# Decoder layer on one core: the G pair of the z blocks moves into the half-product stage, and the convolution of branch C starts there

## What is computed

```python
h = rmsnorm(x, lp['norm_mix'])
z = h @ lp['w_in']
qa, ka, va, qb, fb, ib, gb, xc, gc, xd, gl = jnp.split(z, split_at, axis=-1)
o_a = stick_breaking(qa, k_all, v_all, pos0, lp['sb_bias'])
o_b, S_new = hgrn2(qb, fb, ib, gb, S0, lp)     # o * silu(gb)
o_c, h_new, conv_c_new = rg_lru(xc, gc, conv_c_hist, h0, lp)   # conv, gates, scan, * gelu(gc)
o_d, pool_new = pool_mixer(xd, pool_hist, pos0, lp)
gates = jax.nn.sigmoid(gl.reshape(B, L, N_BRANCH, D_MODEL))
x = x + jnp.sum(gates * proj, axis=2) @ lp['w_out']
```

## Time and profile before

| | |
|---|---|
| median of 3 runs | 1770.21 us (1769.98 to 1774.1) |
| the profiled execution | 1776.43 us |
| its span | 1774.6 us |
| PE busy | 1738.9 us (98%) |
| DVE, ACT, POOL busy | 63%, 41%, 44% |
| granted clock of TensorE, mean | 0.992 of full speed |

### The profile page before, as it was taken

The page is one execution under the profiler, slowest core; times in us unless marked ns, Lnnn a source line. Parts: engine busy times, 40 slices in busy tenths (PEclk is TensorE's granted clock), DMA queues, the critical chain, the costliest instruction groups (busy, mean ns, idle before and its releaser), DMA issues.

```text
span 1774.6 us, 30899 instructions
## 1 busy us (share of the span) xinstructions
PE 1738.9 (98%) x12865; PEld 1686.9 (95%) x12865; DVE 1112.9 (63%) x1255; ACT 730.9 (41%) x1034; POOL 777.4 (44%) x531
## 2 busy tenths in 40 slices
PE   8999999979999999999999999999999999999998
PEld 8999999978999978799999999999999999999998
DVE  6931111836857066657843976888888887775744
ACT  6423332354422266532334654444444443334521
POOL 1656674312222211112133287766777736668021
PEclk9999999989999999999999999999999999999999
DMA  6523326122222532447443222232322285334032
GB/s 226 75 94 111 120 77 215 49 80 66 69 79 80 172 109 93 139 148 260 168 148 111 107 97 98 97 110 103 119 100 97 98 300 184 136 116 146 25 123 97
DMA packets 84655, 214.80 MB, mean 121 GB/s; under 512 B 14851, under 2 KB 31779, under 8 KB 83363
## 3 DMA queue, kind: packets, MB, share of 16 engines
q1 hardware_dynamic: 73570, 189.48, 31.0%
q0 software_dynamic: 4032, 14.68, 2.7%
q10 hardware_dynamic: 6912, 8.65, 1.4%
HBM read 149.48 MB, written 63.40 MB: 120 GB/s over the span
## 4 chain that ended last, share of the span: by engine, by line
PE 90%; DVE 3%; ACT 3%; POOL 2%; DMA 1%; issue 1%; SPq 0%; ACTq 0%; POOLq 0%; DVEq 0%
PE ps L1632 24%; PE ps L1082 20%; PE ps L1069 11%; PE ps L1212 10%; PE ps L1680 10%; PE ps L1664 3%; PE ps L1300 2%; PE ps L1167 1%; PE ps L1385 1%; PE ps L1056 1%; PE ps L1109 1%; DMA masks<-in_wb 1%; PE ps L1549 1%; PE ps L1419 1%; PE ps L1406 1%
## 5 line engine op out<-in xcount | busy, mean ns | idle before, releaser
L3311 POOL TENSOR_TENSOR Wl<-BIG,Wh 128x512 fp32r<-128x512 f32 x110 | 142.9, 1309 | 117.9 <-ACT Wh L2182 117.9
L3166 POOL CAST Uh<-BIG 128x1024 fp32r<-128x1024 f32 x27 | 36.0, 1335 | 310.8 <-PE ps L1069 201.8
L2536 DVE TENSOR_TENSOR BIG<-BIG,ps 128x528 f32<-128x528 f32 x45 | 31.7, 704 | 159.5 <-PE ps L1212 159.5
L2960 DVE SCALAR_TENSOR_TENSOR ps<-BIG,fpar,ps 128x1023 f32<-128x1023 f32 x84 | 107.9, 1285 | 36.0 <-ACT ps L2273 35.1
L1069 PE MATMUL ps<-Hh,Uh 128*128 128x352 f32 x384 | 128.3, 334 | 0.8 <-ACT BIG L1923 0.8
L1069 PE MATMUL ps<-Hh,Ul 128*128 128x352 f32 x384 | 123.6, 322 | 0.0
L1069 PE MATMUL ps<-Hl,Uh 128*128 128x352 f32 x384 | 123.3, 321 | 0.0
L3263 POOL TENSOR_TENSOR Ul<-BIG,Uh 128x1024 fp32r<-128x1024 f32 x15 | 36.1, 2412 | 164.7 <-ACT Uh L2142 164.7
L1632 PE MATMUL ps<-Hl,Wh 128*128 128x264 f32 x528 | 107.1, 284 | 0.0
L1082 PE MATMUL ps<-Hh,Uh 128*128 128x352 f32 x432 | 96.7, 333 | 9.0 <-ACT BIG L1799 6.3
L2949 DVE TENSOR_TENSOR BIG<-BIG,ps 128x528 f32<-128x528 f32 x110 | 77.3, 703 | 42.8 <-PE ps L1632 36.9
(11 more groups left out here) (465 smaller groups left out, 5575.9 us busy)
## 6 DMA issues: line engine op xcount, KB each, us to landing
BIG<-in_wu SPq DMA_DIRECT2D x44, 512.0 KB, 4.6
hidden<-BIG SPq DMA_DIRECT2D x22, 528.0 KB, 2.7
late_gates<-BIG SPq DMA_DIRECT2D x18, 528.0 KB, 3.0
BIG<-sums SPq DMA_DIRECT2D x12, 792.0 KB, 4.8
BIG<-in_wgl SPq DMA_DIRECT2D x9, 1024.0 KB, 5.9
BIG<-in_wd SPq DMA_DIRECT2D x6, 1536.0 KB, 9.6
H<-late_gates SPq DMA_DIRECT2D x17, 528.0 KB, 3.7
gates<-BIG ACTq DMA_DIRECT2D x48, 176.0 KB, 2.1
```

The lines of the kernel that those rows point to most:

```text
L2960: link(v.scalar_tensor_tensor(y[:, back:SEQ], x[:, 0:SEQ - back], w, y[:, back:SEQ], ALU.mult, ALU.add), v.scalar_tensor_tensor(ys[:, :, b ...
L3311: nc.gpsimd.tensor_tensor(Wl[:, b], src, Wh[:, b].bitcast(F32), ALU.subtract).then_inc(S("w_lo"), 1)
```

## The change

- Blocks `GB0` and `GB1` are no longer made by `block_z`. Their weights are the second of now ten pairs (`Z_PAIR = 1`), without the sigmoid; they are stored in `late_gates` and loaded back into `Z` at the stage's end.
- The rows of XC come back into the place of GC (`conv_rows`) and not into that of FB. They are loaded after product T3 of the last pair, and DVE convolves the first row before it adds product T1 of that pair.
- The small tables (histories, `wpool`) lie in `FO` and are loaded while the stage begins. The rows of GC come back after both convolutions.
- ACT's `root(0)` and `gelu(0)` stand ahead of its copies of FB, and `turned_v(0)` ahead of `decay(1)`.
- POOL makes the split of `IB1` ahead of the first pair's seven low parts, not behind three of them.
- Behind the changed places `before()` and `VA0, VA1` keep their order on ACT: `before()` first.

```diff
-ZB = 14
+ZB = 12
+Z_PAIR = 1
-PAIRS = (4 * LATE - COVER) // 2
+PAIRS = (4 * LATE - COVER) // 2 + 1
-         "C10", "C11", "GB0", "GB1", "VA0", "VA1")
+         "C10", "C11", "VA0", "VA1")
...
             def pair_weights(c, sem):
+                if c == Z_PAIR:
+                    src = a["wz"][18:20]
...
+            for i in range(2):
+                sp.dma_start(phist[:, i], a["phist"][i]).then_inc(S("cd_in"), 16)
+            sp.dma_start(chist, a["chist"]).then_inc(S("cd_in"), 16)
+            sp.dma_start(ch0, a["ch0"]).then_inc(S("cd_in"), 16)
+            sp.dma_start(wpool, a["wpool"]).then_inc(S("cd_in"), 16)
...
             sp.wait_ge(*upto("gp_done", made(PAIRS - 1, T3)))
-            rows_back(1, Z[:, XD:XD + 2, :])
-            sp.wait_ge(*upto("gc_kept0", 32))
-            sp.wait_ge(*upto("gc_kept1", 32))
-            rows_back(2, Z[:, GC:GC + 2, :])
+            rows_back(0, conv_rows, on("gw_first"))
+            rows_back(1, Z[:, XD:XD + 2, :], on("gw_in1"))
+            sp.wait_ge(*upto("gp_done", 7 * PAIRS))
...
+            rows_back(3, turn, S("cd_in"))
...
+            sp.dma_start(Z[:, GB:GB + 2, :], late_gates[2 * Z_PAIR:2 * Z_PAIR + 2].rearrange("i p t -> p i t"))\
+                .then_inc(S("cd_in"), 16)
+            sp.dma_start(wrg, a["wrg"]).then_inc(S("cd_in"), 16)
             gate_out(PAIRS - 1, 0)
...
             gate_out(PAIRS - 1, 1)
...
+            sp.wait_ge(S("cd_ready"), 2)
+            rows_back(2, Z[:, GC:GC + 2, :], on("gw_in0"))
...
-            block_z("GB0", (0, lambda: turned_v(0, turn[:, 0], (2,))))
+            block_z("VA0", (0, lambda: turned_v(0, turn[:, 0], (2,))))
             turned_v(1, turn[:, 1], range(2))
-            block_z("GB1", (0, lambda: turned_v(1, turn[:, 1], (2,))))
-            block_z("VA0")
-            block_z("VA1")
+            block_z("VA1", (0, lambda: turned_v(1, turn[:, 1], (2,))))
...
             rates(0)
             decay(0)
+            root(0)
+            gelu(0)
             for i in range(2):
-                act.wait_ge(S("cd_ready"), i + 1)
                 z_out(f"FB{i}", FB[:, i])
...
-            root(0)
-            gelu(0)
             rates(1)
-            decay(1)
             act.wait_ge(S("pool_read"), 2)
             turned_v(0)
+            decay(1)
             root(1)
             gelu(1)
-            z_out("GB0", Z[:, GB, :])
             turned_v(1)
-            z_out("GB1", Z[:, GB + 1, :])
...
+            for c in range(PAIRS):
+                for part in (T2, T3, T1, T4, B22):
+                    if c == PAIRS - 1 and part == T1:
+                        dve.wait_ge(S("cd_in"), 80)
+                        dve.wait_ge(*upto("gw_first", 32))
+                        convolved(0)
+                    gate_sum(c, part)
+            convolved(1)
...
             split(4)
-            for part in LOWS[:3]:
-                gate_low(0, part)
             split(5)
-            for part in LOWS[3:]:
+            for part in LOWS:
                 gate_low(0, part)
```

More of the change, by code:

```diff
@@ L67 @@
 KA = XD
[L68 removed]
+Z_COLS = (1792, 2304, 2048, 1280, 768, 1024, 512, 256, 0, 1536)
 BRANCH_AT = (QA, GB, GC, XD)
@@ L239 @@
 USERS = ("XC0", "XC1", "XD0", "XD1", "GC0", "GC1", "IB0", "IB1", "QB0", "QB1", "C00", "C01", "FB0", "FB1", "D0", "D1",
-         "C10", "C11", "GB0", "GB1", "VA0", "VA1")
-RING = ("XD0", "XD1", "GC0", "GC1", "IB0", "IB1", "QB0", "QB1", "FB0", "FB1", "GB0", "GB1", "VA0", "VA1")
+         "C10", "C11", "VA0", "VA1")
+RING = ("XD0", "XD1", "GC0", "GC1", "IB0", "IB1", "QB0", "QB1", "FB0", "FB1", "VA0", "VA1")
 FRONT = RING.index("IB1") + 1
@@ L394, in program @@
         wrg = r.take(2, 2, P)
-        phist = r.take(2, DB, HIST)
         assert r.at <= R0 + RING_AT - 4 * T
@@ L701, in keep_rows, with rows_back @@
                 outs += 16
-            def rows_back(n, rows):
-                sp.dma_start(rows, early_rows[n].rearrange("i p t -> p i t")).then_inc(S("cd_in"), 16)
+            def rows_back(n, rows, signal):
+                sp.dma_start(rows, early_rows[n].rearrange("i p t -> p i t")).then_inc(signal, 16)
             keep_rows(0, XC)
@@ L743, in _ @@
             sp.wait_ge(*upto("gp_done", made(PAIRS - 1, T3)))
-            rows_back(1, Z[:, XD:XD + 2, :])
-            sp.wait_ge(*upto("gc_kept0", 32))
-            sp.wait_ge(*upto("gc_kept1", 32))
-            rows_back(2, Z[:, GC:GC + 2, :])
-            gate_out(PAIRS - 1, 0)
[L749 to L754, removed]
+            rows_back(0, conv_rows, on("gw_first"))
+            rows_back(1, Z[:, XD:XD + 2, :], on("gw_in1"))
+            sp.wait_ge(*upto("gp_done", 7 * PAIRS))
+            for i in range(2):
+                sp.wait_ge(*upto(f"gc_kept{i}", 32))
+            rows_back(3, turn, S("cd_in"))
+            for half in range(2):
+                sp.wait_ge(*upto(f"g_stored{half}", 16 * (Z_PAIR + 1)))
+            sp.dma_start(Z[:, GB:GB + 2, :], late_gates[2 * Z_PAIR:2 * Z_PAIR + 2].rearrange("i p t -> p i t"))\
+                .then_inc(S("cd_in"), 16)
+            sp.dma_start(wrg, a["wrg"]).then_inc(S("cd_in"), 16)
+            gate_out(PAIRS - 1, 0)
             gate_out(PAIRS - 1, 1)
[L756 to L759, removed]
+            sp.wait_ge(S("cd_ready"), 2)
+            rows_back(2, Z[:, GC:GC + 2, :], on("gw_in0"))
             z_wait("D0")
@@ L814, in gate_in @@
                 i, u = divmod(s, 8)
-                src = gates[i * EARLY + TURN_OF[u] + QKS] if u < EARLY else late_gates[i * LATE + u - EARLY - COVER]
+                n = i * LATE + u - EARLY - COVER
+                src = gates[i * EARLY + TURN_OF[u] + QKS] if u < EARLY else late_gates[n if n < 2 * Z_PAIR else n + 2]
                 sp.dma_start(gate_row(s), src).then_inc(S(gate_loaded(s)[0]), 16)
@@ L1846, in gate_sig @@
                     act.wait_ge(*upto("g_copied", 2 * c + 2))
-                nc.scalar.activation(GY[:, half], GY[:, half], ACT.Sigmoid).then_inc(on("g_sig"), 1)
+                if c == Z_PAIR:
+                    act.sem_inc(on("g_sig"), 1)
+                else:
+                    nc.scalar.activation(GY[:, half], GY[:, half], ACT.Sigmoid).then_inc(on("g_sig"), 1)
             act.wait_ge(S("zc_done"), 2)
@@ L1932, in before @@
                 act.wait_ge(S("d_rows"), 16)
-                for user in ("FB0", "QB0", "GB0"):
+                for user in ("FB0", "QB0"):
                     z_wait(user)
-                for user in ("FB1", "QB1", "GB1"):
+                for user in ("FB1", "QB1"):
                     z_wait(user)
+                act.wait_ge(S("cd_in"), 128)
                 link(nc.scalar.activation(bE, f, ACT.Abs))
@@ L2536, in gate_sum, with convolved @@
                 v.tensor_tensor(quarters(dst), quarters(src), pair(gate_pair(c, b)), ALU.add).then_inc(on("g_sum"), 1)
-            for c in range(PAIRS):
-                for part in (T2, T3, T1, T4, B22):
-                    gate_sum(c, part)
-            dve.wait_ge(S("cd_in"), 160)
-            for i in range(2):
-                x, y = XC[:, i], cX[:, i]
+            def convolved(i):
+                x, y = conv_rows[:, i], cX[:, i]
                 w = [pc("conv_c_w", 2 * j + i) for j in range(4)]
```

22 lines of the change are left out of this document (15 added, 7 removed).

## The result

| kernel | median us (lowest to highest) | executions | profiled: span, clock, its own time |
|---|---|---|---|
| before | 1770.66 (1768.48 to 1775.98) | 13 | 1774.6, 0.992, 1776.43 |
| after | 1777.06 (1773.37 to 1781.59) | 13 | 1775.4, 0.991, 1777.22 |

The ratio is 1.0032, 95% interval 1.0021 to 1.0044: slower by 3.7 to 7.8 us, against a forecast of no change (1769.4). The two profiled executions differ by only +0.8 us of span, 1.6 us from the -0.8 of the sum. So against the one profile that it was made from, the sum came out nearly as worked out, and the number did not. The profiled execution of after lies at the median of its kernel (1777.22 and 1777.06); that of before was taken earlier and lies above all 13 of the row (1776.43). The rest of this text is about that.

What follows compares the result with a forecast made beforehand. PE work was taken as the bound (90% of the chain), with waits and half clock before IB1 and GB0. Terms -2.8 - 5.7 - 13.4 + 7.2 + 1.5 + 12.4 = -0.8 took 1770.2 to 1769.4 us; range 1761.5 to 1775.

Steps and rivals of the forecast that it cites:

- The sum: All six terms added to -0.8 us and subtracted from the median of before, giving 1769.4 us.
- Part 2: In front of IB1: POOL's earlier cast removes PE's wait and the half clock behind it, -5.7 us.
- Part 3: In front of GB0: PE's wait for C's gates goes, 25.20 us become a block and a transpose, -13.4 us.
- Part 6: End of the stretch: ACT's before() delays the VA copies, PE idles some 10 us and its clock falls, +12.4 us.
- Part 1: Fewer matmul columns: one more pair replaces two blocks at full clock, -2.8 us.
- Part 4: Last product of the pairs, B22: waits 4.4 us for rows and convolution, then loses 2.8 to clock, +7.2 us.
- the whole of the 2.8 or none: After a PE gap, the clock has two levels only, so the gap costs all 2.8 us of clock loss or nothing.
- Part 5: QB1's weights: POOL's low part waits for a store now queued behind other transfers, +1.5 us.
- Faster: Rival, chance 0.25: the last product waits little, as rows land fast or the clock holds; 1762 us.
- The slower rival: Chance 0.12: ACT's tail is longer, DVE and POOL collisions start before() later, each us going to PE; 1777 us.

Runs made afterwards that it cites:

- before_new_front: Kernel before with only POOL's order changed, all seven low parts made behind IB1's cast: 1770.16 us, ratio 0.9981 to before.
- conv_behind_sums: Changed kernel with both rows convolved behind all half sums of the last pair: 1772.63 us, ratio 1.0000 to before.
- idle_filled: Changed kernel with 60 added matmuls, results unused, in PE's idle stretch behind VA1: 1774.09 us, ratio 1.0013 to before.

## Why the prediction was wrong, by its own steps

**The step that failed** is in "The sum": "It was 6.2 us above the median; the difference goes with the profile, so I subtract from the median". The difference did not go with the profile in both kernels alike. It was half-clock time and POOL's delay at places that the change rebuilds: IB1, GB0 and the end. Priced in that execution, parts 2 and 3 gained what the median has less of (1.4 to 5.0 us and 0.8 us less in the two later profiles), and part 6 was set against an end that had already lost 2.6 us.

**Part 1, -2.8: right.** Ten pairs took 205.8 us where nothing stands in them, the figure of the forecast.

**Part 2, -5.7.** Right against its profile (105.53 for 106 forecast), too large for the median: 3.4 by `before_new_front`. In the three profiles of before the place offers 5.7, 4.3 and 0.7 us (17.4, 16.0 and 12.4, less one block of 11.7).

**Part 3, -13.4: -12.6.** From the first transposes of V to the last block's end, 61.2 us became 25.2, and 23.4 of that are the two blocks of part 1. Against its own profile (62.0) it was -13.4, as forecast. The mechanism was right.

**Part 4, +7.2: +6.0.** Ten pairs take 211.8 us (105.53 to 317.34) where they take 205.8 without the wait. It is 3.4 us idle for 4.4, since the rows landed in 5.1 us and not in 6.3, then half clock nearly as forecast (5.42 us for a product of 2.94); 4.4 to 5.7 by `conv_behind_sums`. The prediction's "either the whole of the 2.8 or none" did not hold: B22 lost 2.5 us here and 1.3 in `idle_filled`. The Trainium skill (DMA: Bandwidth & Descriptors, Anatomy of one DMA) states its estimate for transfers that GpSimd issues, which the prediction did not say; these are issued by SyncE. It had given 4.5 us, and the row 6.3; the measured 5.1 lies nearer to the estimate.

**Part 5, +1.5: mis-sized.** 2 us of gap, and 13.2 us for QB1 in place of 11.7: +3.5 by the trace, +5.3 by the run that takes it away, with what came of it at the end of the stretch. The gap itself was forecast (1.5, measured 2.0); that the clock would pay for so short a one I had not put in. It did in both profiles of after, and did not in `idle_filled` and `conv_behind_sums`.

**Part 6, +12.4.** +12.5 to `turned_k` against its profile. Of this `before()` itself is 1.2 us, for the 0.8 that I gave to collisions of DVE and POOL. Against an ordinary end it is more: 25.2 us from VA1's end to the first fill (403.63 to 428.82) in place of 10.3: +14.9.

**The sum again**, with these: -2.8 - 3.4 - 12.6 + 6.0 + 3.5 + 14.9 = +5.6 us. Measured: +6.4 by the medians, 3.7 to 7.8 by the interval. By its run part 5 is 1.8 more, which that interval does not exclude.

**The chances.** "Faster" rested on a short landing; it came out shorter than forecast, but its 1.2 us were lost in part 5. The slower rival's mechanism (`before()` starts late by collisions) did not happen: it started 2.1 us behind VA1's start, as forecast, and the one collision cost 1.2 us inside it. That rival's number, 1777, is that of the result, but this is luck: the result came about by another way, which no rival named. (Its terms, three hits of 2 us and 1.7 of the store, make it 6.9 us above before and not 7.5.) What stays open is the last microsecond, behind the first fill, and the 2 to 3 us of `idle_filled`.

## What to carry to other kernels

A sum over one profile is right for that execution. Before it is subtracted from a median, look at how that execution's clock and own time stand among the others, and ask whether the time above the median lies where the change works; if so, it is part of the terms and must not be taken as common to both kernels. A wait that stands in every execution, with PE's clock falling behind it each time, is dearer than one that varies. And look for the wait inside an in-order queue: work that is ready behind it (here the V copies, and the store) can go in front.

## What was not expected of the hardware

- The same program, unchanged, had mean clocks of 0.991 to 0.997 and times of 1767.6 to 1780.7 us, and the time mostly follows the clock (one execution at 0.994 took 1778.75 us).
- A gap of 2.0 us on PE was followed by 3.4 us at half clock (331.32 to 334.7), though the gap's own window had 0.98; gaps of 2.1 us in `idle_filled` and 1.6 in `conv_behind_sums` at the same place by none; gaps of 2.8 us in front of IB1 were followed by 6.0 us at 0.50 in one execution, by a block at 0.87 in another.
- PE at full rate for 9.7 us right ahead of sparse transposes did not keep the clock: from 411.87 to 426.90 it was 0.66, against 0.57 behind 11 us of idling.
- The same store of 528 KB landed within 3.5 us in front of three other transfers and in some 9 us behind them.
